# Choosing the experts of a PEER layer from 54 candidate sums, and a new order of writes at the first value block

## The reference

```python
def peer(h, w_query, sub_keys, expert_u, expert_v):
    ...
    s = jnp.einsum('thcd,hcnd->thcn', q, sub_keys).astype(jnp.float32)
    v1, i1 = lax.top_k(s[:, :, 0], PEER_TOPK)
    v2, i2 = lax.top_k(s[:, :, 1], PEER_TOPK)
    cand = (v1[..., :, None] + v2[..., None, :]).reshape(n_tok, PEER_HEADS, PEER_TOPK * PEER_TOPK)
    best, j = lax.top_k(cand, PEER_TOPK)
    e_idx = (jnp.take_along_axis(i1, j // PEER_TOPK, axis=-1) * PEER_N_KEYS
             + jnp.take_along_axis(i2, j % PEER_TOPK, axis=-1))
    gate = jax.nn.softmax(best, axis=-1)
    ...
        a = jax.nn.gelu(jnp.einsum('cd,chkd->chk', tc, u_sel).astype(jnp.float32), approximate=False)
        w = (gc * a).astype(tc.dtype)
        return jnp.einsum('chk,chkd->cd', w, expert_v[ec])
```

## Time and profile before

| | us |
|---|---|
| median of 3 runs | 1973.65 (1973.49 to 1980.93) |
| profiled execution, its own time | 1973.84 |
| its span, first to last instruction | 1971.9 |
| TensorE busy | 1951.4 (99%) |
| VectorE busy | 1683.8 (85%) |
| ScalarE busy | 1119.8 (57%) |
| GpSimd busy | 719.2 (36%) |

### The profile page before, as it was taken

One profiled execution on the slowest core, in us unless ns is written; L12 is line 12 of the kernel. 1 busy time (PEld: TensorE's weight loads), 2 busy tenths in 40 slices (PEclk: granted clock), 3 DMA queues, 4 the chain that ended last, 5 costly groups with the idle time before them and its releaser, 6 DMA issues. The chain is left out here.

```text
span 1971.9 us, 32481 instructions
## 1 busy us (share of the span) xinstructions
PE 1951.4 (99%) x11706; PEld 1737.4 (88%) x11706; DVE 1683.8 (85%) x2368; ACT 1119.8 (57%) x1585; POOL 719.2 (36%) x406
## 2 busy tenths in 40 slices
PE   9999999999999999999999999999999999999999
PEld 8889989999888888999999999999777777777776
DVE  8777778776877678999999999998888888888887
ACT  7565555555676455666565655655545555555554
POOL 0301111011000001888888888886222222222220
PEclk9999999999999999999999999999999999999999
DMA  6745654565455556999999999999999999999997
GB/s 241 247 159 194 202 192 161 188 204 191 153 177 181 192 182 219 325 312 328 317 325 339 328 305 331 331 401 399 349 376 377 366 380 381 377 367 379 366 385 263
DMA packets 137574, 566.48 MB, mean 287 GB/s; under 512 B 44008, under 2 KB 52080, under 8 KB 88112
## 3 DMA queue, kind: packets, MB, share of 16 engines
q1 hardware_dynamic: 87456, 415.09, 58.2%
q0 software_dynamic: 49776, 148.44, 22.2%
q10 hardware_dynamic: 288, 2.36, 0.3%
HBM read 548.30 MB, written 16.88 MB: 287 GB/s over the span
## 5 line engine op out<-in xcount | busy, mean ns | idle before, releaser
L452 DVE TENSOR_TENSOR wlo<-raw,whi 128x1024 fp32r<-128x1024 f32 x242 | 296.3, 1232 | 109.8 <-PE psum L607 65.5
L873 PE MATMUL psum<-xr,whi 128*128 128x384 f32 x2048 | 382.0, 337 | 0.9 <-ACT whi L458 0.9
L896 PE MATMUL psum<-whi,xr 128*128 128x512 f32 x1512 | 364.0, 389 | 1.0 <-DVE arena L1806 0.6
L873 PEld LDWEIGHTS psum<-xr,whi 128*128 128x128 f32 x2048 | 352.3, 189 | 1.5 <-ACT whi L458 1.2
L896 PEld LDWEIGHTS psum<-whi,xr 128*128 128x128 f32 x1512 | 283.4, 188 | 62.4 <-DVE arena L1806 1.1
L458 ACT ACTIVATE whi<-raw 128x2048 fp32r<-128x2048 f32 x168 | 320.8, 1909 | 21.2 <-DMA raw<-v_rows 10.8
L603 PE MATMUL psum<-xr,whi 128*128 128x512 f32 x1296 | 330.2, 397 | 0.5 <-issue 0.4
L445 ACT ACTIVATE whi<-raw 128x1024 fp32r<-128x1024 f32 x244 | 250.2, 1053 | 107.7 <-DMA raw<-stream 50.9
L1330 POOL DMA_INDIRECT arena<-v_rows,small x64 | 139.2, 2174 | 406.3 <-DVE arena L1764 402.8
L603 PEld LDWEIGHTS psum<-xr,whi 128*128 128x128 f32 x1296 | 232.3, 189 | 44.6 <-issue 1.1
L1335 POOL DMA_INDIRECT gates<-arena x96 | 220.1, 2293 | 29.3 <-issue 29.0
(11 more groups left out here) (284 smaller groups left out, 3248.6 us busy)
## 6 DMA issues: line engine op xcount, KB each, us to landing
raw<-stream SPq DMA_DIRECT2D x244, 512.0 KB, 3.3
raw<-v_rows SPq DMA_DIRECT2D x85, 1024.0 KB, 7.8
raw<-u_cols SPq DMA_DIRECT2D x84, 1024.0 KB, 5.5
arena<-v_rows SPq DMA_DIRECT2D x43, 1024.0 KB, 7.3
arena<-u_cols SPq DMA_DIRECT2D x42, 1024.0 KB, 5.4
gates<-arena POOLq DMA_DIRECT2D x8, 1536.0 KB, 9.8
small<-gates SPq DMA_DIRECT2D x62, 192.0 KB, 8.0
arena<-x_t SPq DMA_DIRECT2D x4, 544.0 KB, 6.6
```

The source lines that it names most:

```text
L452: nc.vector.tensor_tensor(wlo[:, k % 2 * HALF:(k % 2 + 1) * HALF], raw[:, s * HALF:(s + 1) * HALF], f(whi[:, s * HALF:(s + 1) * HALF]), AL ...
L873: mm(bank(at, 0, 2 * TD), hi_w[:, c * P:(c + 1) * P], z_all[:, :, c, 0:TD // TS, :], start=c == 0, stop=False)
L896: last = mm(at[:, (b * 4 + j * 2 + n) * 512:(b * 4 + j * 2 + n + 1) * 512], weights, src, start=begin, stop=end, skip_group_check=True)
```

## The change

There are two parts.

The first is in `route`. If both lists of 16 scores are sorted, the sum of score a of one and score b of the other can be among the best 16 only if (a+1)(b+1) is at most 16. `PAIR_ROWS` names five rectangles that hold these pairs, 54 in all. Steps 4 and 5 search the 54 sums and not 256. Beside each sum stands a key: a number whose high bits tell the place of the pair among the 54 and whose low bits tell the expert. The winner's place is made into the same form, and the exclusive or of its bits with every key, with the minimum over the 54, leaves the expert's number. Before, the number was gathered by comparing with 0 to 15, a product and a sum over 512 elements.

The second part is at the first value block: TensorE first does all that goes to banks 0 and 1 and to banks 4 to 7 with the high parts, and only then what goes to banks 2 and 3. VectorE takes the last two expert sums one by one, and no longer together.

```diff
@@ -80,7 +80,10 @@
 
 CONSTS = [("mean2048", P), ("eps", 1), ("rope_cos", T + L), ("rope_sin", T + L), ("mask", SC_W), ("mean64", P),
           ("mean128", P), ("ident", P), ("one", 1),
-          ("iota16", TOPK), ("token", 2), ("coef", 4)]
+          ("place", 2 * TOPK), ("token", 2), ("coef", 4), ("stride", 2)]
+PAIR_ROWS = [(0, 1, 16, 0), (1, 1, 8, 16), (2, 2, 5, 24), (4, 4, 3, 34), (8, 8, 1, 46)]
+CAND = 54
+PLACE_UNIT, PLACE_ORIGIN = float(1 << 14), float(1 << 23)
 FIRST_CONSTS = P + 1
 PARAMS = [("g_mix", KC), ("g_peer", KC), ("b_gate", 2 * KC), ("g_dq", 1), ("g_dk", 1), ("g_fq", 1), ("g_fk", 1),
           ("g_sub", 1), ("b_forget", 1), ("lambdas", 256), ("w_forget", KC * HEADS), ("sub_keys", HEADS * NK)]
@@ -123,8 +126,12 @@
     put("ident", np.eye(P))
     dense = (np.arange(T) < TD).reshape(2, P).T
     put("token", np.where(dense, np.arange(T).reshape(2, P).T, 0))
-    put("coef", np.stack([np.where(dense, NK * TD, 1), np.where(dense, TD, NK)], 2).reshape(P, 4))
-    put("iota16", np.arange(TOPK)[None, :])
+    put("coef", np.stack([np.where(dense, NK, 1), np.where(dense, 1, NK)], 2).reshape(P, 4))
+    put("stride", np.where(dense, TD, 1))
+    begin = np.zeros(TOPK)
+    for a, height, width, first in PAIR_ROWS:
+        begin[a:a + height] = first + width * np.arange(height)
+    put("place", np.concatenate([PLACE_ORIGIN + PLACE_UNIT * begin, PLACE_UNIT * np.arange(TOPK)])[None, :])
     put("eps", EPS)
     put("one", 1.0)
     return c
@@ -284,9 +291,13 @@
         def lists(w):
             return late.take(w * TOPK).rearrange("p (c m) -> p c m", c=w)
 
-        idxs, idxf, vals, jf = (lists(2) for n in range(4))
-        idxu, jh = (lists(2).bitcast(U32) for n in range(2))
-        best, index, gate_exp = (late.take(TOPK) for n in range(3))
+        pair = late.take(4 * TOPK).rearrange("p (q c m) -> p q c m", q=2, c=2)
+        vals, idxs = pair[:, 0], pair[:, 1]
+        idxu = lists(2).bitcast(U32)
+        ju_place = late.take(TOPK)
+        differ = late.take(TOPK * CAND).bitcast(U32).rearrange("p (k n) -> p k n", k=TOPK)
+        best, gate_exp = (late.take(TOPK) for n in range(2))
+        index = late.take(TOPK).bitcast(U32)
         ju = late.take(TOPK).bitcast(U32)
         neg_best, gate_sum = late.take(1), late.take(2)
         mixed = [late.take(2 * TOPK).rearrange("p (z m) -> p z m", z=2) for h in range(HEADS)]
...
@@ -299,15 +310,15 @@
...
-        iota16 = few[:, 0:TOPK]
-        token = [few[:, TOPK + b:TOPK + b + 1] for b in range(2)]
-        coef = [few[:, TOPK + 2 + 2 * b:TOPK + 4 + 2 * b] for b in range(2)]
-        few_from = C["iota16"]
-        few_at = c_at["iota16"][0]
-        few_from = c_sb[:, few_at:few_at + TOPK + 6]
+        cands = small[:, 512:512 + 2 * CAND].rearrange("p (q n) -> p q n", q=2)
+        cand, cand_key, cand_left = cands[:, 0], cands[:, 1], small[:, 768:768 + CAND]
...
@@ -902,16 +913,21 @@
                 if first:
                     pe.wait_ge(bank_free, F_V)
                 part(0, 0, psum, Whi[q][:, 0:P], False, first, False)
-                if first:
-                    pe.wait_ge(bank_free, 2 + F_V)
-                part(0, 1, psum, Whi[q][:, 0:P], False, first, False)
+                if not first:
+                    part(0, 1, psum, Whi[q][:, 0:P], False, False, False)
                 pe.wait_ge(w_lo, base + c + 1)
                 if first:
+                    part(0, 0, psum, Wlo[q][:, 0:P], False, False, False)
                     pe.wait_ge(row_used, ROWS)
-                if residual is None:
+                    for j in range(2):
+                        part(1, j, psum, Wboth[q], False, True, False)
+                    pe.wait_ge(bank_free, 2 + F_V)
+                    for weights in (Whi[q], Wlo[q]):
+                        part(0, 1, psum, weights[:, 0:P], False, weights is Whi[q], False)
+                elif residual is None:
                     for j in range(2):
                         part(0, j, psum, Wlo[q][:, 0:P], False, False, False)
-                        part(1, j, psum, Wboth[q], False, first, False)
+                        part(1, j, psum, Wboth[q], False, False, False)
                 else:
                     part(0, 0, psum, Wlo[q][:, 0:P], False, False, False)
                     part(0, 1, psum, Wlo[q][:, 0:P], False, False, False)
@@ -1714,10 +1730,14 @@
                 if m == 3:
                     V.max_index(idxu[:, 1, 8:16], vals[:, 1, 8:16], sc_left[:, 1, :]).then_inc(sc_taken, 1)
                     dve.wait_ge(sc_taken, t + 2)
-                    V.tensor_tensor(idxs, idxu, spread(coef[b].unsqueeze(2), 2, TOPK), ALU.mult)
-                    ch.link(V.tensor_tensor(cand.rearrange("p (a b) -> p a b", a=TOPK),
-                                            spread(vals[:, 0, :].unsqueeze(2), 2, TOPK),
-                                            spread(vals[:, 1, :].unsqueeze(1), 1, TOPK), ALU.add), True)
+                    V.scalar_tensor_tensor(idxs[:, 0], idxu[:, 0], coef[b][:, 0:1], place[:, 0], ALU.mult, ALU.add)
+                    ch.link(V.scalar_tensor_tensor(idxs[:, 1], idxu[:, 1], coef[b][:, 1:2], place[:, 1],
+                                                   ALU.mult, ALU.add))
+                    for a, height, width, at in PAIR_ROWS:
+                        to = cands[:, :, at:at + height * width].rearrange("p q (a b) -> p q a b", a=height)
+                        last = V.tensor_tensor(to, spread(pair[:, :, 0, a:a + height].unsqueeze(3), 3, width),
+                                               spread(pair[:, :, 1, 0:width].unsqueeze(2), 2, height), ALU.add)
+                    ch.link(last, True)
                 if m == 4:
                     ch.link(V.max(best[:, 0:8], cand), True)
                     V.max_index(ju[:, 0:8], best[:, 0:8], cand)
@@ -1725,17 +1745,15 @@
                 if m == 5:
                     ch.link(V.max(best[:, 8:16], cand_left), True)
                     ch.link(V.max_index(ju[:, 8:16], best[:, 8:16], cand_left))
-                    V.tensor_scalar(jh[:, 0, :], ju, 4, None, ALU.logical_shift_right).then_inc(best_ready, 1)
-                    ch.link(V.tensor_scalar(jh[:, 1, :], ju, TOPK - 1, None, ALU.bitwise_and))
+                    V.tensor_scalar(ju_place, ju, PLACE_UNIT, PLACE_ORIGIN, ALU.mult, ALU.add).then_inc(best_ready, 1)
                 if m == 6:
-                    ch.link(V.tensor_tensor(eq, spread(jh.rearrange("p c k -> p k c").unsqueeze(3), 3, TOPK),
-                                            spread(spread(iota16.unsqueeze(1).unsqueeze(1), 1, TOPK), 2, 2),
-                                            ALU.is_equal))
+                    dve.wait_ge(best_ready, t + 1)
+                    ch.link(V.tensor_tensor(differ, spread(ju_place.bitcast(U32).unsqueeze(2), 2, CAND),
+                                            spread(cand_key.bitcast(U32).unsqueeze(1), 1, TOPK), ALU.bitwise_xor))
                 if m == 7:
-                    ch.link(V.tensor_tensor(eq, eq, spread(idxs.unsqueeze(1), 1, TOPK), ALU.mult))
-                    ch.link(V.tensor_reduce(index, eq.rearrange("p k c m -> p k (c m)"), AX.X, ALU.add))
+                    ch.link(V.tensor_reduce(index, differ, AX.X, ALU.min))
                     at = mixed[h][:, 0, :] if b else pick_at[h]
-                    V.tensor_scalar(at.bitcast(U32), index, token[b], None, ALU.add)
+                    V.tensor_scalar(at.bitcast(U32), index, stride[b], token[b], ALU.mult, ALU.add)
                 if m == 8:
                     gate = mixed[h][:, 1, :] if b else pick_gate[h]
                     dve.wait_ge(best_exp, t + 1)
@@ -1799,6 +1817,11 @@
                 dve.wait_ge(w_hi, chunk + 1)
                 V.tensor_tensor(Wlo[q], W[:, chunk, :], f(Whi[q]), ALU.subtract).then_inc(w_lo, 1)
 
+            def expert_sum(n):
+                dve.wait_ge(half_done, 2 * F_U + 2 * n + 2)
+                dve.wait_ge(low_part, n + 1)
+                V.tensor_tensor(W[:, n, :], bank(U_BANKS[n % 4], 0, TD), W[:, n, :], ALU.add).then_inc(bank_free, 1)
+
             def expert_sums(n):
                 dve.wait_ge(half_done, 2 * F_U + 2 * n + 4)
                 dve.wait_ge(low_part, n + 2)
@@ -1808,6 +1831,8 @@
             for n in range(B_U):
                 if n and n % 2 == 0:
                     expert_sums(n - 2)
+                if n == B_U - 1:
+                    expert_sum(n - 1)
                 step(2 * n)
                 step(2 * n + 1)
                 if n < B_U - 1:
@@ -1815,7 +1840,7 @@
                 if n == B_U - 2:
                     gate_weights(0)
             weight_lo(0)
-            expert_sums(B_U - 2)
+            expert_sum(B_U - 1)
             lo_block(dve, B_U)
             gate_weights(1)
             def bank_residual(n):
```

(20 more changed lines are left out.)

## The result

The change is slower: 1984.49 us in the median (20 executions, 1974.15 to 1989.48) against 1975.78 before, a ratio of 1.004, interval [1.003, 1.0049]. I had forecast 1970.2 us, a gain of 3.6. The profiled execution took 1980.05 us; all of its readings are against the one of before, 1973.84 us, so they account for 6.2 us and not for the 8.7 between the medians.

The account below looks back on a forecast made before the run. TensorE, busy 1951.4 of 1971.9 us, was taken as the bound. Gains of 3.2 us in the expert stage and 0.4 at the value stage, 3.6 off 1973.84, gave 1970.2 us; range 1965.5 to 1978.0.

Parts of the forecast that it names:

- VectorE's saving: Expert stage: shorter routes free 0.7 us of VectorE each, 10 us over 14 routes, bounds 1 and 13.
- the sum: Whole kernel: 3.2 us from the expert stage plus 0.4 from the value stage, 3.6 us off 1973.84.
- a crowding of 6.3 us: Expert stage: TensorE time that VectorE's load of routes can have lost, 4.5 us plus 1.8 given as (3.7 - 1.87).
- step 3 grows: VectorE's routes: this step of each route was to get longer by some 0.8 us.
- the products at a granted clock of 0.66: Expert stage, TensorE: a clock fall over 4.5 us about doubled the pace of products; about 1.7 us lost.
- The value block: Value stage start: the reordered products and separately taken sums gain TensorE 0.4 us, bounds 0 and 0.8.
- the new wait at the low part: Value stage: after 12 products TensorE waits about 0.5 us for VectorE's low part of the value weights.
- I take half, 3.2 us, between none and all: Expert stage: half of the 6.3 us loss returns, because GpSimd has no slack and its fetches come late.
- the third rival: Expert stage: GpSimd loses six of 256 instructions, rows come 14 us later, about 1982 us; 15%.
- its clock term: Expert stage: in the case where GpSimd falls back, 1.7 us for a second fall of TensorE's clock.
- its signs: Expert stage: GpSimd's last fetch moving from 1361 us by over some 4 us, or more clock falls, would refute the prediction.
- The rival's account, by gaps that hold three or one: Expert stage: about three GpSimd instructions fit between low parts after a row product, otherwise one; shorter steps shorten the three-instruction gaps.

Follow-up runs that it names:

- route_only: Kernel before with only the changed routes, keeping the old value block: 1981.97 us, ratio 1.0029.
- after_shift: Changed kernel with every step of routes 2 to 15 one place later in VectorE's list: 1984.29 us, ratio 1.0041.
- after_xor2: Changed kernel with its exclusive or of 864 elements done twice: 1981.52 us, ratio 1.0042.
- before_shift: Kernel before with every step of routes 2 to 15 one place later in VectorE's list: 1975.09 us, ratio 0.9998.
- after_early: Changed kernel with row fetches 12 steps ahead of use where it had 8, rows 3 to 45: 1974.31 us, ratio 0.9992.
- after_wide: Changed kernel with its five searches over 240 columns where it has 54: 1972.69 us, ratio 0.9979.

## Why the prediction was wrong

**VectorE's saving, right in the main.** 10 us were forecast for the 14 routes of the stage; 8.2 show there in the pair without writes and 9.6 over all 16 routes with them, 0.6 us per route for 0.7. Once the rows are never late, 3.6 us of it reach TensorE, against the 3.2 of the sum. That these agree is partly luck: the sum took half of a crowding of 6.3 us, and the kernel without writes shows 5.0, of which most goes. Two details of the text are off and carry nothing: step 3 grows by 0.6 us by its own terms and not 0.8, and the products at a granted clock of 0.66 took about 1.4 times their time (4.12 us for 2.97) and not double.

**The value block, right.** 0.39 us for 0.4, with the new wait at the low part that the text names (0.31 us for about 0.5).

**The step that failed** is "I take half, 3.2 us, between none and all". In the sum GpSimd's pace could only withhold the gain; that it might fall was put at nothing there. But it fell: its 256 instructions now take 775.9 to 1370.4 us, 2.32 us each for 2.28, 9.7 us more in all. In place of a gain of 3.2 us the 127 blocks took 8.3 us more: 6.6 of stalls and 5.1 of the clock, less 3.4 saved. This was the third rival, "GpSimd falls back", which had 15%, with rows 14 us later, 7 us of stalls, 1.7 for the clock and 1982 us. So its way was right, and its clock term a third of what was measured. The case came with its signs: row waits of 21.2 us for 8.1, the last fetch at 1369.4 us for 1361.4, three falls of the clock for one.

That rows made late by GpSimd are the way is shown: earlier fetches alone take 10 us off the changed kernel, and without the writes the change is a gain of 4.4 us. That TensorE's clock took 5.1 us of it is read from one profiled execution of each kernel. Other profiles vary: by windows of 5 us the clock takes 6.8 us of this stage in `route_only` and 5.1 in `after_shift`, but 1.7 in `after_xor2` and 3.4 in `before_shift`, which is not slow; in `after_early`, `after_wide` and the two without writes it takes none.

**Why its pace fell** is narrowed down. The low parts hold as many of its instructions as before, each for longer (100.6 us for 94.1). It is not VectorE's load (1 us more per route in step 6 leaves the time within 3.5 us of the changed kernel's, none slower), not the second input (1.5 us), not the place of the steps by one, not the width of the searches as such. Giving time to steps 4 and 5 restores it, whether by wider searches or idle instructions. Taking time from these steps in the kernel before raised the hold by 2.7 us and did not bring its time up, so short steps 4 and 5 alone are not the whole cause; the rest of the change (steps 3, 6 and 7) has a part in it, and which of them was not tried. Why GpSimd's instructions come to begin earlier in the low parts is open. The rival's account, by gaps that hold three or one, fits what was measured but no run tests it.

**A write under the exclusive or.** It is held as by a low part, in the timelines of VectorE and GpSimd of the changed kernel:

```profile
1089.03 1.05 DVE L1751 TENSOR_TENSOR arena<-arena,small 128x864 uint32<-128x864 uint32 x1
...
1089.25 2.27 POOL L1351 DMA_INDIRECT gates<-small  x1 [0.30 <-issue]
```

The exclusive or ends at 1090.08, and the write 1.44 us later, as in the earlier trace rows. The Trainium skill (SBUF — State Buffer, "Who interferes with whom") says that a VectorE instruction with two inputs in SBUF contends with a GpSimd instruction that reads SBUF; the trace agrees for the short instruction too. The prediction has GpSimd shut out for the whole length of such an instruction; the section says of it only that it contends, and the length is what the traces show. The hold does not carry the time: twice the exclusive or cost no more than twice the minimum, 1981.5 and 1981.1 us.

## What to carry to other kernels

An engine that is 37% busy over the kernel can be saturated for the stage that counts. Look at its idle gaps there (0.30 us, every one) before counting a saving on another engine as a gain, and when a fetched operand stands in front of a critical instruction in program order, first give the fetch more lead. The fastest complete kernel here keeps the new choice of experts and gives steps 4 and 5 their length back (0.9979 of before, and so without the saving); none was found that has both the saving and rows in time to the end.

## What was not expected of the hardware

Less work on VectorE made GpSimd slower, with no instruction of GpSimd changed: 146 for 150 in the same 355 us. Every low part held one of its instructions, and what changed was for how long. And short stalls of TensorE cost about twice their length when the clock follows: idle 2.43 us, then 9 us at a granted 0.62, where a stall of 2.16 us near 944 us of the same execution left the clock alone, as this pair of timeline rows of TensorE shows (the products after it keep their usual 2.97 us):

```profile
943.96 2.03 PE L889 MATMUL psum<-xr 128*128 128x192 f32 x16 [2.16 <-DVE xr L480]
945.83 2.97 PE L884 MATMUL psum<-xr,whi 128*128 128x384 f32 x16
```
